# Layer 1's memory keys and values, moved from layer 0's routing to the end of layer 0, in a decoder step on one Trainium2 core

## The reference, cut to what matters

```python
for l in range(DEPTH):
    ...
    mk, mv = mem_kv(mem_prompt, w_mem_k[l], w_mem_v[l])
    mem_k_p.append(mk)
    mem_v_p.append(mv)
    xp = layer_norm(ALPHA * xp + mem_attend(xp, mk, mv, w_mem_q[l], w_mem_o[l]), ln_g[l, 1], ln_b[l, 1])
    ...
def mem_kv(mem, w_k, w_v):
    B, M, _ = mem.shape
    return (mem @ w_k).reshape(B, M, MEM_HEADS, MEM_HEAD_DIM), (mem @ w_v).reshape(B, M, MEM_HEADS, MEM_HEAD_DIM)
```

## Time and profile before

| What | us |
|---|---|
| median of three runs (1067.45 to 1069.46) | 1069.1 |
| the profiled execution: its time | 1067.35 |
| its span, from first to last instruction | 1065.7 |
| PE busy in the span (91%) | 970.7 |
| DVE busy (49%) | 521.7 |
| ACT busy (33%) | 353.8 |
| POOL busy (23%) | 244.4 |
| layer 0's expert stage, from the first turning to the last product | 443.8 to 589.6 |

### The profile page before, as it was taken

How to read it: one execution, slowest core, us unless ns; L and a number is a source line. 1 busy time by engine, 2 the same in 40 slices (tenths; PEclk the granted TensorE clock), 3 DMA queues, 4 the chain that set the end, 5 groups by cost and what they waited for, 6 DMA issues and landing times.

```text
span 1065.7 us, 17849 instructions
## 1 busy us (share of the span) xinstructions
PE 970.7 (91%) x6998; PEld 599.4 (56%) x6998; DVE 521.7 (49%) x1078; ACT 353.8 (33%) x881; POOL 244.4 (23%) x290
## 2 busy tenths in 40 slices
PE   7999999998989998899999398999899887999995
PEld 6877778887446757633333156657548663333332
DVE  0246520467657657343232455684178584333327
ACT  2334531121011624233333344554214332333423
POOL 2550000051500001435410005500000015352121
PEclk9999998999999988999999699899999976999998
DMA  9636102072207234989999503441146145999978
GB/s 321 174 107 218 40 1 79 1 198 80 69 0 202 78 161 176 416 310 409 410 412 344 196 1 84 95 153 41 59 140 277 40 159 206 344 395 408 417 225 197
DMA packets 78027, 203.60 MB, mean 191 GB/s; under 512 B 19096, under 2 KB 44352, under 8 KB 68848
## 3 DMA queue, kind: packets, MB, share of 16 engines
q1 hardware_dynamic: 61568, 153.44, 39.6%
q0 software_dynamic: 16368, 48.93, 14.6%
HBM read 184.46 MB, written 25.92 MB: 197 GB/s over the span
## 4 chain that ended last, share of the span: by engine, by line
PE 76%; DVE 11%; DMA 5%; ACT 4%; issue 3%; POOL 0%; SPq 0%; DVEq 0%; POOLq 0%; ACTq 0%
PE PS L1615 15%; PE PS L1418 11%; PE PS L1056 8%; PE PS L1157 6%; PE PS L1632 6%; PE PS L1441 3%; ACT arena L1996 2%; PE PS L1765 2%; DMA x<-y_tok 2%; PE PS L1121 2%; PE PS L1840 2%; PE PS L1599 2%; PE PS L1079 2%; PE PS L1850 2%; PE PS L1044 1%
## 5 line engine op out<-in xcount | busy, mean ns | idle before, releaser
L1996 ACT ACTIVATE arena<-PS 32x520 f32<-32x520 f32 (+9 forms) x150 | 73.8, 503 | 184.5 <-PE PS L1056 43.2
L1615 PE MATMUL PS<-ring,arena 128*32 128x512 f32 x648 | 116.9, 593 | 1.4 <-DVE arena L3058 1.4
L1615 PE MATMUL PS<-arena 128*32 128x512 f32 x648 | 112.5, 610 | 3.0 <-issue 2.0
L1056 PE MATMUL PS<-xT,ring 128*128 128x260 f32 x416 | 95.2, 390 | 4.5 <-DVE arena L2486 3.1
L3074 DVE COPY arena<-PS 128x256 f32<-128x256 f32 x24 | 10.2, 425 | 170.0 <-PE PS L1623 170.0
L1056 PEld LDWEIGHTS PS<-xT,ring 128*128 128x128 f32 x416 | 79.5, 193 | 19.3 <-DVE arena L2486 5.1
L2280 ACT ACTIVATE arena<-PS,lnc 128x128 f32<-128x128 f32 x184 | 66.8, 468 | 35.5 <-PE PS L1599 35.5
L1632 PE MATMUL PS<-ring,arena 128*32 128x512 f32 x432 | 69.0, 595 | 1.2 <-DVE arena L3074 1.2
L826 POOL TENSOR_TENSOR rstd<-rstd,small 128x1 f32<-128x1 f32 (+1 forms) x20 | 12.6, 628 | 243.8 <-DVE rstd L2774 243.8
L1157 PE MATMUL PS<-ring,xT 128*128 128x256 f32 (+2 forms) x336 | 67.9, 364 | 0.0
L1615 PEld LDWEIGHTS PS<-arena 128*32 128x32 f32 x648 | 30.0, 112 | 60.8 <-issue 56.5
(11 more groups left out here) (440 smaller groups left out, 1838.0 us busy)
## 6 DMA issues: line engine op xcount, KB each, us to landing
arena<-in_moe_w_in_dram SPq DMA_DIRECT2D x27, 1024.0 KB, 9.4
ring<-in_moe_w_in_dram SPq DMA_DIRECT2D x27, 1024.0 KB, 11.7
ring<-in_moe_w_out_dram SPq DMA_DIRECT2D x18, 1024.0 KB, 11.1
ring<-in_w_in_even_dram SPq DMA_DIRECT2D x11, 1024.0 KB, 11.2
xT<-in_moe_w_in_dram SPq DMA_DIRECT2D x10, 1024.0 KB, 11.1
arena<-in_moe_w_out_dram SPq DMA_DIRECT2D x8, 1024.0 KB, 13.2
xT<-in_moe_w_out_dram SPq DMA_DIRECT2D x6, 1024.0 KB, 14.2
y_tok<-in_c_zeros_dram POOLq DMA_DIRECT2D x8, 512.0 KB, 10.9
```

The lines of the kernel that those rows point to most:

```text
L1056: mm = pe.matmul(o[out_rows, 512 * h:512 * h + HALF], lhs(k), rhs(k)[:, HALF * h:HALF * h + HALF], start=(k == 0), stop=(k == nk - 1))
L1615: mm = pe.matmul(o[group(q), 0:512], xT_[:, k, group(q)], w(q, k), start=(k == 0), stop=(k == KD - 1), **quarter(q))
L1996: return act.activation(dst, src, ACT.Copy)
```

## The change

Layer 1's memory work leaves layer 0's routing. Its two weight pieces stand behind all of layer 0's expert pieces in `W`, and go to arena slots; the memory tokens are loaded ahead of them. Each half of the tokens is turned behind T of one of the last two blocks. Three of the four runs (keys and values of the first half, keys of the second) stand in a branch for a spill count of zero, ahead of the spill branch, and once more at the end of the spill branch. The last run (values of the second half) stands between the turnings of tile 0 and tile 1; mkT stands behind the second input product. `mk[1]` moves from `cosf` to the arena columns that the query halves (`qnT`) use later, so their copies wait for `moe_done`, which POOL raises once the memory stores have landed; POOL issues these stores behind its power for tile 0. In `expert_rows` SP waits for the turned tokens ahead of tile 3's rows and for the last run ahead of tile 4's.

```diff
-LATENT_IN = [("xT", 2, 0), ("xT", 2, 1), ("oin", 0), ("xT", 2, 2), ("oin", 1), ("xT", 2, 3), ("oinT", 0), ("oin", 2),
+LATENT_IN = [("xT", 2, 0), ("mkV",), ("xT", 2, 1), ("oin", 0), ("xT", 2, 2), ("oin", 1), ("mkT", 1), ("xT", 2, 3), ("oinT", 0), ("oin", 2),
...
-            jobs += LATENT_PE
+            jobs += [("mkv", 1, 0), ("mkv", 1, 1)] + [key for key in LATENT_PE if key != ("mkV",)]
...
-            jobs += [("memF", 1, 0), ("memF", 1, 1), ("rank", 0), ("mkv", 1, 0), ("table", 0), ("mkv", 1, 1)]
+            jobs += [("rank", 0), ("table", 0)]
...
-        if l == 0:
-            memory_pieces(1)
         pieces = []
...
             piece(*rest)
+        if l == 0:
+            memory_pieces(1)
...
+        if name in (("mk", 1), ("mv", 1)):
+            slots = range(SLOTS, SLOTS + EXTRA_SLOTS)
...
-        mk = (part(2, 256, at0=4 * T), cosf[:, 0:512].rearrange("p (a b) -> p a b", a=2))
+        mk = (part(2, 256, at0=4 * T), part(2, 256, at0=3648))
...
                 for t in range(NT):
+                    if t >= NT - 2:
+                        full(sp, (("memF", 1, 1), ("mkv", 1, 1))[t - NT + 2])
                     for c in range(2):
...
-                if l == 0:
-                    memory_out(1)
-                else:
+                if l:
                     pool.wait_ge(s["cleared"], 16 * 9)
...
                         power(rms[0:ROWS[t], t % 2, 2:4])
+                        if t == 0:
+                            memory_out(1)
...
             def experts(l):
-                if l == 0:
-                    for m in range(2):
-                        memory_features(1, m)
                 key = ("rank", l)
...
-                if l == 0:
-                    memory_keys_values(1, 0, (0,))
                 key = ("table", l)
...
                 block_sums(0, "dest_sums")
-                if l == 0:
-                    memory_keys_values(1, 0, (1,))
...
                 block_sums(1, "gate_sums")
-                if l == 0:
-                    memory_keys_values(1, 1, (0,))
                 pe.wait_ge(s["gate_rows"], l + 1)
                 close(block_table(1), key)
-                if l == 0:
-                    memory_keys_values(1, 1, (1,))
...
-                    if (l, st_, b) == (0, "X", 1):
-                        memory_keys_back(1)
+                    if l == 0 and st_ == "T" and b >= BLOCKS_M - 2:
+                        memory_features(1, b - (BLOCKS_M - 2))
...
-                if l:
-                    with pe.If(spill_count == 0):
-                        held_blocks()
+                with pe.If(spill_count == 0):
+                    held_blocks() if l else memory_behind_blocks()
...
+            def memory_behind_blocks():
+
+                memory_keys_values(1, 0)
+                memory_keys_values(1, 1, (0,))
...
                 act.activation(st[0:1, 26:27], small[0:1, EPSILON:EPSILON + 1], ACT.Sqrt)
+                take_memory(("mkv", 1, 0))
                 for t in range(2):
...
                 act.activation(st[0:1, 26:27], small[0:1, EPSILON:EPSILON + 1], ACT.Exp)
+                act.wait_ge(s["moe_done"], 1)
                 for j in (1, 3):
...
+                dve.wait_ge(s["moe_done"], 1)
                 for j in (0, 2):
```

More of the change, by code:

```diff
@@ L288, in psum_jobs @@
         for s, b in block_order():
-            jobs += [("moe" + s, l, b)] + ([("mkT", 1)] if (l, s, b) == (0, "X", 1) else [])
+            jobs += [("moe" + s, l, b)] + ([("memF", 1, b - (BLOCKS_M - 2))] if l == 0 and s == "T" and b >= BLOCKS_M - 2 else [])
     jobs += [("cmb", t) for t in LAST_TILES]
@@ L525, in decoder_step @@
         assert at[0] <= ARENA - EXTRA_SLOTS * PIECE
-        y_front = part(3, 2, D, at0=4096)
+        y_front = part(3, 2, D, at0=4160)
         y_of = [y_front[:, t] for t in range(3)] + [pbuf, pT]
@@ L538, in decoder_step @@
         qn_at = at[0]
+        assert qn_at == 3648
         qnT = part(4, T)
@@ L706, in load_piece @@
                     released(before)
-                if slot >= SLOTS + EXTRA_SLOTS:
+                if name[0] in ("mk", "mv"):
+                    pass
+                elif slot >= SLOTS + EXTRA_SLOTS:
                     full(sp, ("rt", name[1]))
@@ L883, in dispatch @@
                         if l == 0:
-                            pool.wait_ge(s["stored"], 16 * n_stored[0])
-                            full(pool, ("mkT", 1))
                             load(kvg[:, :], io["mla_kv_norm"][0].partition_broadcast(P), "odd_in")
@@ L1689, in experts @@
                     taken(pe, ("moeT", l, BLOCKS_M - 1))
+                    if l == 0:
+                        taken(pe, ("memF", 1, 1))
                     pe.wait_ge(sem_["table_in"], 1)
@@ L1725, in experts @@
                         held_blocks()
+                    else:
+                        pe.wait_ge(sem_["act"], 3 * SPILL)
+                        memory_behind_blocks()
+            def memory_behind_blocks():
+                memory_keys_values(1, 0)
+                memory_keys_values(1, 1, (0,))
             def held_blocks():
@@ L1789, in query_half @@
                         close(mm, key)
-                steps = {"xT": transpose_x, "oin": oin, "oinT": oin_back, "ukT": latent_keys, "qn": lambda j: query_half(j, 0)}
+                steps = {"mkV": lambda: memory_keys_values(1, 1, (1,)), "xT": transpose_x, "oin": oin, "oinT": oin_back, "ukT": latent_keys, "qn": lambda j: query_half(j, 0),
+                         "mkT": memory_keys_back}
                 for key in LATENT_PE:
@@ L2267, in experts @@
                     act.activation(v, v, ACT.Exp).then_inc(s["router_exp"], 1)
-                    if (l, n) == (0, 0):
-                        for m in range(2):
-                            take_memory(("memF", 1, m))
                 for v, name in enumerate(("dest", "gate")):
@@ L2273, in experts @@
                     copy(table_rows[:, v, :], pair(("table", l))[:, 512 * v:512 * v + P]).then_inc(s[name + "_rows"], 1)
-                    if l == 0:
-                        take_memory(("mkv", 1, v))
                 def gained_rows(o, dst, chunks=range(KD)):
@@ L2325, in experts @@
                     steps[st_](b)
-                    if (l, st_, b) == (0, "H", 0):
-                        take_memory(("mkT", 1))
+                    if l == 0 and st_ == "T" and b >= BLOCKS_M - 2:
+                        take_memory(("memF", 1, b - (BLOCKS_M - 2)))
                 sem_ = spill_s[l]
@@ L2385, in latent_attention @@
                     row_root(2, t, t)
-                steps = {"xT": turned, "oin": latent_squares, "oinT": back,
+                steps = {"mkV": lambda: take_memory(("mkv", 1, 1)), "mkT": lambda l: take_memory(("mkT", l)), "xT": turned, "oin": latent_squares, "oinT": back,
                          "ukT": lambda: take(("ukT",), ukT, lambda o: o[:, 0:512].rearrange("p (c q) -> p c q", c=4))}
```

## The result

| | before | changed |
|---|---|---|
| median, us (20 runs each) | 1068.26 (1061.32 to 1074.28) | 1071.57 (1068.01 to 1074.38) |
| ratio, 95% interval | | 1.0032 [1.0018, 1.0046] |
| the profiled execution: time, span | 1067.35, 1065.7 | 1069.59, 1067.9 |

The change makes the kernel slower, by 0.32% (some 3.4 us); the forecast was 1067.4 us with 1063.6 to 1070.6 as its range. The profiled executions stand 2.24 us apart. They can be laid beside each other mark by mark: the changed kernel is ahead up to one place in layer 1's head, and what it loses there is more than its lead.

What follows compares the result with a forecast made beforehand. The prediction took PE (TensorE), with 76% of the chain of waits, as the bound. Its terms summed to -1.72 us: 1065.6 us in the profiled execution, 1067.4 as the median, range 1063.6 to 1070.6.

Steps and rivals of the forecast that it cites:

- 1. Routing: Layer 0's routing: without the memory work the table and gather come earlier, gather time kept at 8.71 us; -3.97 us.
- rival C: Layer 0's gather: the routing's gain stays in the DMA queue, leaving 0.6 or 2.3 us; sum 0.0, 1069.1 us; chance 0.13.
- 2. Cold first block: Layer 0's first expert block: without the removed runs PE's clock is low, as in layer 1's; +2.86 us.
- Rival B: Layer 0's first block isn't cold, the clock returning amid routing's small matmuls; sum -4.6, 1064.5 us; chance 0.12.
- 3. The keys' turning: Four transposes move from behind the first hidden product to behind layer 1's second input product; 0, within 0.6 us.
- 4. Memory turnings: Between T and Y of layer 0's last two blocks: turning the memory tokens costs 2 x 0.28 = +0.56 us.
- 5. Three megabytes at the end: Layer 0's end: memory tokens and two weight pieces load hidden, tokens by only 1.2 us; the last scatter slows; +0.5 us.
- Rival D: Before Y of block 10: memory tokens land late and PE waits, +5.2 us; sum +3.5, 1072.6 us; chance 0.10.
- 6. Three runs in idle PE: End of layer 0: three memory runs, 11.1 us, fit in PE's idle time before layer 1's first turning; 0.
- 7. Head: Layer 1's head: tile 1's turning and product 0 at full clock, -3.07 us; a slow stretch after the remaining gap, +1.4.
- 8. New waits: Layer 1: query copies waiting for moe_done, tile 4's rows for the fourth run, and ScalarE's values copy cost nothing; 0.
- E. The way out of the branch: After the three runs PE's jump over the spill branch takes 6 us; sum +0.8, 1069.9 us; chance 0.03.

Runs made afterwards that it cites:

- experiment 6: experiment 1 plus identity transposes nothing reads, ahead of layer 0's first block's turning: with 24, 1064.51 us (0.9956 of before); with 42, 1060.98 us (0.9938).
- experiment 4: experiment 1 with the fourth memory run also in the no-spill branch, instead of between tile 0's and tile 1's turnings: 1070.09 us, 1.0003 of the kernel before.
- experiment 5: experiment 4 with its four memory runs taken out of the branch and placed behind the spill branch: 1068.00 us, 0.9994 of the kernel before.
- experiment 1: The changed kernel with mkT behind input product 0 instead of product 1: 1064.18 us, 0.9952 of the kernel before; on another chip 1063.90 us, 0.9963.
- 7, with 36: experiment 1 plus 36 unread identity transposes ahead of tile 0's turning at layer 1's head: 1066.54 us, 0.9975 of the kernel before.
- with 16 transposes: experiment 1 plus 16 unread identity transposes ahead of tile 0's turning at layer 1's head: 1064.49 us, 0.9955 of the kernel before.
- experiment 2: The kernel before plus an empty job of four identity transposes behind input product 1, copied by ScalarE: 1076.58 us, 1.0072 of the kernel before.
- experiment 3: The kernel before plus an empty job of four identity transposes behind input product 0, copied by ScalarE: 1069.27 us, 0.9996 of the kernel before.

## Why the prediction was wrong, point by point

The sum was -1.72 us in the profiled execution, and +2.24 was measured. The steps one by one:

- *1. Routing, -3.97:* measured -5.27 at the first turning. The table came as priced from layer 1 (10.56 against 10.47). The gather, kept at 8.71 us, took 7.51; the bound "0 if it lands when it did" and rival C, the gain staying in the queue, were both wrong.
- *2. Cold first block, +2.86:* measured +1.79 in the changed kernel. Pricing it by layer 1's block was right in kind and 1.1 us high here; experiment 6 puts it at 1.9 to 2.4 and shows its cause. The rule drawn from the Trainium skill ("TensorE: Matmul & The Clock Gate", What's actually happening), that the throttled state is the default, agrees with the trace: 24 transposes brought 1.00, and 2.58 us of idleness later it was 0.50 again. Rival B is false.
- *3. The keys' turning, 0 within 0.6: this is the step that failed.* In the old place its four transposes did come off the path (from the first block's second half to T of block 10 128.87 us against 129.43, 0.56 less), and 0.44 us came on in the new one. But the step counted PE's time alone. Moving a job in `LATENT_IN` moves the pair of every job behind it, and for product 2 the fourth job back became product 1. That costs 4.65 us of waiting and 3.28 us of low clock, 7.9 us together, more than the whole gain. The trace of before doesn't show that wait, but it holds what was needed: counting four jobs back in the new list leads from product 2 to product 1, and before, product 2 began at 626.3 where DVE let product 1's pair go at 631.3.
- *4. Memory turnings, +0.56:* from T of block 10 to Y of block 11 6.08 us against 5.60, +0.48.
- *5. Three megabytes at the end, +0.5:* the last output product to tile 0's turning took 17.77 us against 18.29, so 0.5 us less, not more. The tokens, issued at 558.2, landed after 16.7 us at 574.9, 1.6 us before they were wanted (1.2 forecast). Rival D, the slower case, is false; that its time, 1072.6, lies near the measured median says nothing for it.
- *6. Three runs in idle PE, 0:* right. They start with no gap behind the last product (585.83, 10.63 us) and 3.64 us of idleness follow, where 3.5 to 3.9 were forecast.
- *7. Head, -3.07 and +1.4:* tile 1's turning and product 0 take 6.47 us against 9.54, -3.07; tile 0's to tile 1's turning 6.27 against 4.81, +1.46, with the clock at 0.50 from 602 to 604. Both as forecast. Rival A is false.
- *8. New waits, 0:* right for the semaphores that the change adds. The wait that came was an old one with a new partner.
- *E. The way out of the branch:* shows nothing in the changed kernel, where 3.64 us of idleness lie behind the runs. Its size was doubted too much: experiments 4 and 5 show 4.5 to 6.3 us in two spells. The step "in layer 1 PE enters such a branch with no idle time" looked at the way in, not the way out.

So the forecast was wrong twice, in opposite directions. At tile 2's turning the sum had -1.72 and the trace has -5.69: the gather gave 1.3 more, the cold block cost 1.1 less, the end of layer 0 was 1.1 better, the keys' old place gave 0.6. Behind it came the wait that no step had. Without it -5.69 + 0.44 = -5.25 us would be left, and experiment 1, the same kernel without the wait, is 5.1 us faster than the kernel before (0.0048 of 1069.4) on one chip and 4.0 on the other. That these lie near 5.25 is in part luck: in the trace of the second run product 2 starts only 2.94 us ahead of before, since 2.3 us less were won ahead of it than in the changed kernel, 1.1 of them because tile 1's rows landed later (below), and the whole span is 3.7 us shorter. One entry in a list turned a gain of 4 to 5 us into a loss of 3.4.

## What to carry to other kernels

Where buffers go round in a fixed order, a job that is moved or added changes the partner of every job behind it: for each of them count back to the job whose buffer it takes over, and ask when that one is emptied, before costing the move at its own busy time. Put small jobs where the buffer that falls to the next long job was last held by something short-lived. And ask what an idle gap hides (a jump, a late tile) before filling it.

## What the runs showed of the hardware that was not expected

- After PE jumps over a long branch it can stand without instructions in two spells: 2.51 and 3.82 us (experiment 4), 3.11 and 1.36 (5), 1.62 and 1.21 (7, with 36); with 16 transposes only the first shows, 2.22 us. Each ends 2.4 to 2.6 us behind a 16 KB piece in the instruction queue (experiment 5). They can only be seen when work is queued behind the jump.
- A wait costs PE twice: behind 4.65 us of idleness the product ran at 0.50 for most of its length, 8.87 instead of 5.59 us, and in experiment 2, behind 4.61 us, it took 7.41.
- Behind the last scatter SP loads the tiles' rows in pieces of 512 KB. The first two, tile 0's, land after 3.5 to 3.7 and 4.4 to 4.7 us in every trace. The third, tile 1's first, lands after 5.3 to 5.6 us in before, the changed kernel and experiment 3, but after 6.1 to 7.0 in all the others. DVE then waits for it (1.54 us in the second run of experiment 1), and tile 0's norm stands behind that wait in DVE's order: the last output product to tile 0's turning takes 18.86 us there against 17.77 in the changed kernel. Experiments 2 and 3 differ in nothing that SP or POOL issue (6.3 and 5.5 us), so the order of work doesn't explain it. With one trace of each kernel, chance isn't ruled out either; what sets it is open.
